# Encoder block on eight cores: the head of the projection phase is reordered, the constants are fetched in its fourth chunk, and the norm of a tile is split in two steps

## The reference

```python
h = rms_norm(x, norm_g)
u, g_pool, q, k, v, g_na = split(h @ w_in)            # 1024 -> 6 x 1024
pool_out = pool_mixer(u, w_pool, pool_scale) * silu(g_pool)
na_out = neighborhood_attention(q, k, v, rpb, meta_bias) * silu(g_na)
y = rms_norm(x + concat(pool_out, na_out) @ w_out, final_g)
```

## Time and profile before

| | |
|---|---|
| median of 3 runs | 1771.95 us (1765.36 to 1772.95) |
| profiled execution | 1772.99 us, span of its slowest core (core 3) 1771.5 us |
| spans of the eight cores | 1756.9 to 1771.5 us |
| PE busy | 1697.0 us, 96% |
| DVE busy | 1001.9 us, 57% |
| ACT busy | 821.2 us, 46% |
| share of PE in the chain that ended last | 79% |
| DMA | 287.63 MB, mean 162 GB/s |

### The profile page before, as it was taken

One profiled execution on the slowest core, in us unless ns is written; L12 is line 12 of the kernel. 1 busy time (PEld: TensorE's weight loads), 2 busy tenths in 40 slices (PEclk: granted clock), 3 DMA queues, 4 the chain that ended last, 5 costly groups with the idle time before them and its releaser, 6 DMA issues.

```text
span 1771.5 us, 39313 instructions; the slowest of 8 cores (1756.9 to 1771.5 us)
## 1 busy us (share of the span) xinstructions
PE 1697.0 (96%) x13906; PEld 875.6 (49%) x13906; DVE 1001.9 (57%) x1907; ACT 821.2 (46%) x1219; POOL 114.7 (6%) x186
## 2 busy tenths in 40 slices
PE   7799999999999999999999889899999999999998
PEld 3344544444455555555555554344444444444443
DVE  3354544442466675666667665456655566556654
ACT  3356666331266765677666662223333233323332
POOL 1011021111100000000000110000000000000000
PEclk9899999999999999999999999899999999999999
DMA  9689778653555566666533448853466336642421
GB/s 249 228 221 291 228 238 240 199 169 137 171 138 156 147 177 177 150 185 180 148 108 107 151 133 235 217 140 102 105 173 173 100 92 154 173 138 98 111 95 60
DMA packets 157446, 287.63 MB, mean 162 GB/s; under 512 B 63235, under 2 KB 85251, under 8 KB 148679
## 3 DMA queue, kind: packets, MB, share of 16 engines
q1 hardware_dynamic: 106103, 157.66, 31.3%
q0 software_dynamic: 34880, 91.46, 18.8%
q10 hardware_dynamic: 16272, 35.99, 6.6%
HBM read 193.33 MB, written 100.90 MB: 166 GB/s over the span
## 4 chain that ended last, share of the span: by engine, by line
PE 79%; DMA 6%; ACT 4%; issue 4%; SPq 3%; DVE 3%; ACTq 0%; DVEq 0%; POOL 0%; POOLq 0%
PE bankpair L427 17%; PE bankpair L403 9%; PE bankpair L612 8%; PE bankpair L889 8%; PE bankpair L580 8%; PE bankpair L376 8%; PE bankpair L908 8%; PE bankpair L1016 4%; PE bankpair L985 4%; ACT sb_PT L991 2%; DMA at_s<-sb_ATT 2%; DMA sb_XSG<-xt 1%; SPq L471 1%; SPq L350 1%; PE bankpair L1004 1%
## 5 line engine op out<-in xcount | busy, mean ns | idle before, releaser
L991 ACT ACTIVATE sb_PT<-bankpair 128x1024 bf16<-128x1024 f32 (+1 forms) x368 | 318.9, 921 | 162.7 <-PE bankpair L985 105.8
L427 PE MATMUL bankpair<-sb_Wo,sb_MIX 128*128 128x512 bf16 x1536 | 333.6, 379 | 0.0
L427 PEld LDWEIGHTS bankpair<-sb_Wo,sb_MIX 128*128 128x128 bf16 x1536 | 150.2, 98 | 181.5 <-issue 0.7
L997 DVE TENSOR_TENSOR sb_PT<-sb_PT,sb_FT 128x1024 bf16<-128x1024 bf16 (+1 forms) x264 | 175.4, 667 | 114.0 <-ACT sb_PT L991 111.5
L908 PE MATMUL bankpair<-sb_Wz,sb_HT 128*128 128x512 bf16 x768 | 201.3, 386 | 3.6 <-ACT sb_PM L934 2.8
L580 PE MATMUL bankpair<-sb_HT,sb_Wk 128*128 128x512 bf16 (+1 forms) x832 | 191.2, 385 | 8.3 <-ACT sb_Wk L215 3.9
L889 PE MATMUL bankpair<-sb_HT,sb_Wq 128*128 128x512 bf16 x768 | 191.8, 380 | 1.9 <-DVE sb_QT L213 1.7
L376 PE MATMUL bankpair<-sb_HT,sb_Wg 128*128 128x512 bf16 x768 | 186.4, 387 | 5.9 <-DVE sb_Y L430 4.7
L612 PE MATMUL bankpair<-sb_Wv,sb_HT 128*128 128x512 bf16 x816 | 184.0, 379 | 0.0
L433 ACT ACTIVATE sb_junk<-sb_Y 128x1024 bf16<-128x1024 f32 x48 | 50.7, 1056 | 273.4 <-DVE sb_Y L430 273.4
L403 PE MATMUL bankpair<-sb_HT,sb_Wg 128*128 128x512 bf16 x768 | 167.7, 379 | 0.0
(11 more groups left out here) (103 smaller groups left out, 1707.2 us busy)
## 6 DMA issues: line engine op xcount, KB each, us to landing
sb_X<-xall SPq DMA_DIRECT2D x51, 512.0 KB, 6.6
sb_XR<-xall SPq DMA_DIRECT2D x48, 512.0 KB, 5.2
y<-sb_O POOLq DMA_DIRECT2D x48, 512.0 KB, 4.9
sb_HT<-hT_s SPq DMA_DIRECT2D x23, 1024.0 KB, 6.7
sb_KR<-kT_s SPq DMA_DIRECT2D x14, 1024.0 KB, 7.7
sb_UW<-u_s SPq DMA_DIRECT2D x54, 256.0 KB, 7.7
kT_s<-sb_KTs POOLq DMA_DIRECT2D x13, 1024.0 KB, 5.0
v_s<-sb_Vs POOLq DMA_DIRECT2D x49, 260.0 KB, 3.6
```

The source lines that it names most:

```text
L427: S.op('tensor', lambda e, po=po, kc=kc, cg=cg, j=j: e.matmul(banks[po][:, :], MIX[:, kc, j * 128:(j + 1) * 128], Wo[kc // 4][:, kc % 4, c ...
L991: S.op('scalar', lambda e: e.activation(out=PT[ps][0:nk, bi, :, 0:n].rearrange('p (a b) q -> p a b q', a=2), in_=bank2[sp][0:nk, :].rearra ...
L997: S.op('vector', lambda e: e.tensor_tensor(out=PT[ps][0:nk, bi, :, 0:n], in0=PT[ps][0:nk, bi, :, 0:n], in1=bl['E'](hs), op=ALU.mult), read ...
```

## The change

In the head, K of chunk 0 starts without waiting for the second half of the work on it; K of chunk 1 leaves the head and is done inside the loop, between the transposes of chunk 2 and V of chunk 1, as it is for all later chunks. Chunk 0's half 0 of V comes right after its K, with the last transposes of chunk 1 between, and its half 1 at the end. The four casts of Wv stand together ahead of these. `p1_keep(0)` moves behind K of chunk 0. Ten warming matmuls go. `p1_consts` moves from the head to the start of the chunk at index 3. `p1_front` is split into `p1_sum` (ACT) and `p1_scale` (DVE): in the loop a tile's sum of squares is made two tiles ahead of its transpose and its scaling one tile ahead; before, both came one tile ahead.

```diff
-                def p1_front(ci, j):
+                def p1_sum(ci, j):
...
+
+                def p1_scale(ci, j):
+                    xs, sc = tile_xs[(ci, j)], tile_sc[(ci, j)]
                     S.op('vector', lambda e, sc=sc: e.reciprocal(rstd[:, sc:sc + 1], sd[:, sc:sc + 1]),
                          reads=[('sd', sc)], writes=[('rstd', sc)])
...
+                def p1_front(ci, j):
+                    p1_sum(ci, j)
+                    p1_scale(ci, j)
...
                 for i in range(4, 8):
                     p1_weight(i)
-                p1_consts()
+                p1_wcast(0)
+                p1_wcast(1)
+                p1_K(0, [0, 1])
+                p1_wcast(2)
+                p1_front(1, 0)
+                p1_K(0, [2, 3])
+                p1_wcast(3)
+                p1_front(1, 1)
+                p1_K(0, [4, 5])
+                p1_T(1, 0)
+                p1_K(0, [6])
+                p1_HTevac(1, 0)
+                p1_front(1, 2)
+                p1_T(1, 1)
+                p1_K(0, [7])
+                p1_HTevac(1, 1)
+                p1_front(1, 3)
                 p1_keep(0)
-                p1_wcast(0)
+                for i in range(4, 8):
+                    p1_wcast(i)
+                p1_sum(2, 0)
+                p1_T(1, 2)
+                p1_VU(0, 0, (0,))
+                p1_HTevac(1, 2)
+                p1_T(1, 3)
+                p1_scale(2, 0)
+                p1_VU(0, 1, (0,))
+                p1_HTevac(1, 3)
+                p1_VU(0, 2, (0,))
+                p1_sum(2, 1)
+                p1_VU(0, 3, (0,))
                 for j in range(4):
-                    if j < 3:
-                        p1_wcast(j + 1)
-                    else:
-                        p1_front(1, 0)
-                        p1_front(1, 1)
-                    p1_K(0, [2 * j, 2 * j + 1])
-                for j in range(4):
-                    p1_T(1, j)
-                    if j < 2:
-                        p1_front(1, j + 2)
-                        p1_warm(5)
-                    p1_HTevac(1, j)
-                    p1_wcast(4 + j)
-                p1_keep(1)
-                for j in range(4):
-                    p1_K(1, [2 * j, 2 * j + 1])
-                    if j == 2:
-                        p1_front(2, 0)
-                for j in range(4):
-                    p1_VU(0, j)
+                    p1_VU(0, j, (1,))
...
-                    if idx > 1:
-                        p1_keep(ci)
+                    p1_keep(ci)
+                    if idx == 3:
+                        p1_consts()
                     for j in range(4):
                         if j < ntn:
                             p1_T(nxt, j)
                             if (nxt, j) in after:
-                                p1_front(*after[(nxt, j)])
-                        if idx > 1:
-                            p1_K(ci, [2 * j, 2 * j + 1])
+                                p1_scale(*after[(nxt, j)])
+                                if after[(nxt, j)] in after:
+                                    p1_sum(*after[after[(nxt, j)]])
+                        p1_K(ci, [2 * j, 2 * j + 1])
```

## The result

The changed kernel takes 1778.77 us in the median of 9 runs (1775.22 to 1785.65), the kernel before 1768.60 us in 9 runs beside them (1764.79 to 1777.97). The ratio is 1.0055, interval [1.0034, 1.0077]: slower, by 6 to 14 us, where the prediction said 19 and put 1773 to 1800 around it. Slower by over 0.5% was given 0.70; the measured ratio is just over that line and its interval reaches to both sides of it. Some kernels of the experiments had executions in a second, slower state of the chip, and their medians and ratios here are of the others.

A forecast was written before the change was run, and what follows sets the result against it. The prediction took the head as bound by the DMA engines and the loop by PE. On 1772.99 us, - 2.0 + 20.4 + 2.9 - 0.9 - 1.7 = + 18.7 gave 1791.7, as a median 1791; range 1773 to 1800.

The forecast's parts named there:

- The head: Start of the first phase: load 7 lands at 57.1 us, PE resumes at 59.8, index 2 starts at 104.6; gain 2.0 us.
- the bound of 49 us for the landing: Head: earliest landing of load 7, if both stores come too late to disturb; 57.1 us was forecast.
- The wait at index 3: PE's second transpose of index 3 waits 20.4 us behind DVE's halving of psc; bounds 13.6 and 25.9 us.
- I take 160.5: Index 3: assumed landing time of psc in us, between HT's store at 162.9 and its own issue at 142.3.
- the small wait that went: Index 3: PE's existing wait of 0.87 us at 158.94 goes, counted as 0.9 us of gain.
- Wp's and flg's users come ... tens of us later: Constants fetched at index 3: their users come at index 4 and 6, so no wait was added for them.
- The reason for the delay: Index 3: psc stands in POOL's queue behind HT's store, which landed 24.1 us after issue, and cannot overtake it.
- The split: Loop's norm, sum two tiles ahead and scaling one: reciprocals stop waiting for roots; gain 1.7 us, bounds 0 and 9.
- The base: Whole kernel: the profiled 1772.99 us to which all terms were added; the median of the runs lies 1.0 lower.
- a quick landing of psc: Rival at index 3: psc lands at 146.5 us, PE waits 6.4 us, total 1775.5 us; chance 0.15.
- A head that gains 8 us more, beside a full wait: Rival: load 7 lands at 49 us, waits at 250 us go whole, 7 more; total 1776 us; chance 0.15.
- the first rival: psc lands quickly at index 3; a landing before 150.5 us keeps the result within 0.5%; chance 0.15.

The follow-up runs named there:

- e1: Changed kernel with psc's halving moved to index 5, the constants still fetched at index 3; ratio 1.0013 to the kernel before.
- e9: Changed kernel with psc's DMA on POOL's queue ahead of HT's store and the other constants; one execution, index 3 takes 43.5 us against 48.2.
- e4: Changed kernel with psc's DMA issued on ACT's queue instead of POOL's; one execution, index 3 takes 42.4 us against 48.2.
- e5: Changed kernel with the constants fetched at index 1 and psc halved at index 5; 1760.47 us, ratio 0.9951 to the kernel before.
- e7: e5 with the whole norm, sum and scaling, one tile ahead again; 1765.06 us, ratio 0.9974 to the kernel before.
- e2: Kernel before with only the call of p1_consts, fetch and halving, moved to index 3; ratio 1.0082 to the kernel before.

## Why the prediction was wrong in size

The sign was right, and so was the place of the loss: DVE stuck on psc's DMA, and PE behind it. The sum was + 18.7 us and the phase moved by + 11.5, the ratio says + 6 to + 14. The measured median stands inside the range and the move was half of the forecast. Of the 7.2 us between sum and phase, 3.8 lie at index 3, 2.4 in the head and 1.1 in the split (rounded); the rest of the kernel came out another 2.8 us shorter, without a cause that a run shows.

- **The head.** Gain 2.0 forecast, 4.4 measured. On core 0 it went as worked out: cast 7 at 57.08 (57.1 forecast), PE resuming at 59.58 (59.8), index 2 at 104.33 (104.6). But that is a late core, and the hit is partly luck: cast 7 starts at 54.9 us in the mean, and in the kernel before the prediction had read core 3. On core 3 load 7 had landed by 48.85, PE stood 2.15 us in place of 10.29, and index 2 started at 94.99. In the kernel before, where every core starts index 2 between 104.2 and 108.0, I could not see that the cores would part; the bound of 49 us for the landing was reached by a core.
- **The wait at index 3: the step that failed.** "I take 160.5": the landing of psc, set 2.4 us ahead of a store of HT that took 24.1 us to land on core 3, as what the stall relieves. That gave 18.2 us from psc's issue to its landing and a wait of PE of 20.4 us. It was 13.5 to 16.0 us, and PE waited 15.2 to 18.0 us, 16.5 in the mean, with 2.3 us of slow matmuls on top, 2.9 forecast. Together with the small wait that went it is 18.6 for 22.4. The stall's relief was sized far too small: e1, with the halving moved away and nothing else, puts it at 12 us for psc (27.0 to 14.7 in the mean). HT's store landed after 14.0 to 16.8 us where it took 20.1 to 24.5 without the stall (e1), Wp after 15.0 to 17.2 where it took 31 to 38. The wait shortens itself. On core 0 POOL and ACT issued nothing between Wp's DMA and 160 us, where e1 issued three V stores and one pair of table loads; which of them gives the room isn't separated. That only 3.5 us of the landing are left in the end is partly luck: the rows of the kernel before, with no constants in the line, put psc 20.6 to 24.1 us after its issue, too early against the 27.0. Core 3 pushed the other way, with the slowest HT store of all; on the other cores of the kernel before it took 20.1 to 23.1 us.
- **"Wp's and flg's users come ... tens of us later", so nothing:** wrong, and that the sum didn't feel it is luck. On core 0 of e1 the fold stood ready 29 us after Wp's issue and Wp took 31.9 to land; with psc out of the way Wp costs 7.8 us at index 4 in the mean. It fell out of the changed kernel's time only because the larger wait covers it.
- **The reason for the delay.** The prediction laid it on the line in POOL's queue. The order of landing bears it out on all cores, but its price is open: HT's store and the five constants ahead of psc make 1.3 us in the mean under the stall (e9), kT's store and WuT stayed ahead, and a queue with only table loads in it was as late (e4). The Trainium skill (DMA: Bandwidth & Descriptors, Issuing engines are not separate DMA queues) says that DMAs started by different engines run on the same 16 DMA engines and interleave; the trace of e4 agrees, psc by ACT taking 13.9 to 16.8 us. Its fit of about 2.0 us plus bytes over 436 GB/s for one DMA (same page, Anatomy of one DMA) gives an estimate of some 2 us here. The shortest landing of psc in any of these runs is 9.6 us (e5), nearly five times that, and the measurement decides.
- **The split.** 1.7 forecast, 2.8 measured in the budget, 3.6 by e7 against e5. The reciprocals in the 250 us stretch no longer wait for roots, but HTevac still comes late behind the copies: PE waited 1.61, 2.42 and 1.86 us for it on core 0, and once 1.24 us for a reciprocal, to be read beside the earlier trace rows.
- **The base.** All was added to core 3's execution of 1772.99 us, the slowest of the cores shown. The term that varies from core to core is not carried by the slowest one of before: in the changed profile it was core 0, and core 3 the second fastest. A change of the mean over the cores, 1762.5 to 1771.2 or + 8.7 in the profiled executions, is near to the ratio's 9.7 us, where the single cores say from - 7.1 (core 3) to + 17.2 (core 4).

The rivals: a quick landing of psc was wrong: no core landed it under 12 us in any of the kernels that fetch it at index 3, and DVE's wait was there in full. A head that gains 8 us more, beside a full wait, came true on core 3 alone (index 2 at 95.0 us); cores 5 and 6 went half of the way (100.4 and 99.9), and the other five stayed within 2.5 us of the forecast. That is where the 2.4 us come from by which the mean of the head is over the forecast. One slip in the first rival moves nothing: a landing at 150.5 us makes a wait of 10.4 us, not 10.6.

## What to carry to other kernels

Moving a fetch out of a crowded head means moving whatever consumes it too: a tiny operation that only prepares a value for much later stands in order on its engine and turns the fetch's latency into a stall of everything behind it. Put the fetch where the windows show room in the DMA engines, and above all the consumer several chunks later; here that turned a loss of 0.55% into a gain of 0.5%, and with the last casts and the first stores out of each other's way 1.0%. And when a wait is taken away, look for the one it was hiding. Size a wait from all cores rather than from the slowest, and don't size a new stall from landings on a core that runs: the stall can hold back the traffic that delays it.

## What the runs showed of the hardware

A DMA of 4 KB took 12.0 to 18.3 us to land in a stretch in which the DMA engines were busy throughout and the core stalled, on either of two queues (changed, e2, e4, e9). On a running core it took 22.4 to 30.1 us there (e1), and 9.6 to 14.6 us at index 1 (e5). The windows of core 0 over the wait, of the changed kernel and then of e1 (the last figures are granted clock, DMA share and GB/s):

```profile
138.00:156.00 18.00, 3.26 (x16) 1.27 (x13) 0.00 (x0) 1.93 (x4) 4.77 (x9) 0.66 1.04 245
```

```profile
138.00:156.00 18.00, 18.00 (x103) 8.79 (x102) 8.31 (x13) 11.52 (x18) 4.66 (x8) 1.00 1.02 299
```

The share is full in both, so the share doesn't tell how long a DMA issued now will take.

The same DMA of Wp landed 14.8 to 17.6 us after its issue at index 1, 15.0 to 17.2 us in a stalled core at index 3, and 31 to 38 us in a running core at index 3. With the shorter stalls of e9 and e4 it took 20.1 to 21.3 and 21.3 to 25.9 us. In the head of the changed kernel the cast that waits for the last weight load started between 49 and 58 us on the eight cores of one execution, where the program is the same on each.
